# Trainium2, a two-block model on one core: in the seven-product projections the fifth product's low weight part made by VectorE, with other orders and the softmax scaling on ScalarE

## The chip, the cores and the metric

One core of one Trainium2 chip. The metric is the device time of one execution in microseconds (us); lower is better.

## The reference

Input x is 512 tokens by 2048 features. A first block (RWKV heads, pooled means, stick-breaking attention) and two further layers follow, then a last RMS norm. The change touches the last of these layers and the step behind it:

```
def odd_layer(x, norm_g, w_in, b_forget, w_out):
    hn = rmsnorm(x, norm_g)
    q, k, v, z, f_logit = split(hn @ w_in)
    log_f = log_sigmoid(f_logit + b_forget)
    o = forgetting_attention(q, k, v, log_f)     # 16 heads of 128
    o = o * silu(z)
    return x + o @ w_out
```

Per head, forgetting attention is softmax(q k^T / sqrt(128) + decay, causal) times v.

## The kernel before, in words

Everything is fp32. A product of a weight tile and the activations is made of three TensorE products: each operand is split into a high part (rounded to fp32r) and a low part (the rest), and high·high, low·high and high·low are added in PSUM. ScalarE makes a weight's high part (a copy, "cast" below), GpSimd or VectorE its low part (a subtraction of two tiles in SBUF, 128x1024; GpSimd does it as two instructions of 128x512).

In the odd layer, heads 1 to 15 get their four columns q, k, v, z by a block scheme with seven products instead of eight (`W7_`, lines 1930 to 2190). A **pair** is two of the four columns: the first pair (`pp` 0) is q and k, the second (`pp` 1) v and z. A pair has four weight blocks b11, b21, b12, b22 and seven products P0 to P6 (`w7_product`, matmuls at L2080, L2082 and L2083). Below, a name with a dash (P2') is of the second pair. The weights of the products are made in place, by these steps, each named in the code:

- `T1` to `T4` (L2147, L2151, L2153, L2157; VectorE): the sums of blocks that products 1, 2, 4 and 6 take.
- hi 0 to hi 6 (L2097, ScalarE): the casts. Cast 1 needs T1, cast 2 T2, cast 4 T3, cast 6 T4.
- low parts `l1`, `l2` on VectorE (L2163); lo 0, 3, 4, 5, 6 on GpSimd in that order (`w7_gpsimd`, L2174). T1 overwrites b11, so that it waits for lo 0.
- results: `x1`, `x5`, `x2`, `c21` (ScalarE, L2107, L2110, L2113, L2116) and `c12`, `c22`, `c11` (VectorE, L2129, L2132, L2135). P2 waits for x1, P3 for x5, P4 for x2, P5 for c12, P6 for c22: they leave the PSUM bank that the next product adds to.

A **unit** is one head's attention with the next head's two pairs woven in (`attention_tensor`, `attention_scalar`, `attention_vector`, lines 2193 to 2491); there are 15 units with products and a last one without. Every engine's order is written out by hand. TensorE's is: scores s (L2225), P0, transposes of v (`vt`, L2202), P1 to P4, the transposes of the softmax (`tp`, L2236), P5, P6, the output product (`pv`, L2244), P0' to P6'. VectorE's is: T2, the decay added to the scores and the mask (L2389, L2393), T3, l2, the row maxima (`largest`, L2399), T4, then `scaled`: v's low part `vl` (L2404), the reciprocal `rec` (L2406) and four multiplications of the exponentials by it (`sc0` to `sc3`, L2410); c12, c22, `pl` (L2414), T1', c11, l1', T2', T3', l2', `mix` (the head's gated output, L2422), T4', four steps that split q and k (`qh` to `kc`, L2381 and L2382), c12', c22', the next unit's T1, c11', l1. ScalarE's order is: cast 2, cast 3, x1, `vn` (L2268), x5, casts 4 and 5, four exponentials (L2274), x2, cast 6, cast 0', `pt` (L2279), cast 1', c21, casts 2' and 3', a wait for `mix` and the DMA that stores it (L2312), x1', cast 4', x5', cast 5', x2', cast 6', the next unit's cast 0, Silu (L2332), the next unit's cast 1, c21'.

The transposes `tp` wait for sc3. Weight blocks come by DMAs on SyncE's queue (`w7_sync`), each behind the step that frees its buffer.

Before unit 0, the activations of the products are summed (`fold_sums`) and split (`fold_round`, `fold_rest`, L1923); their low parts were made by VectorE for sums 1 and 3, by GpSimd for 2 and 4. Behind the last unit's products, two output tiles start early (`gemm_two`, L362 to L364, called by `early`): four weight parts cast by ScalarE (L2023), their low parts made by GpSimd (`out3_gpsimd`, L2031).

Of the kernel before, what the change touches and what calls it, by code (L numbers as in the profile page):

```python
# [181 lines left out]
def build_program(nc, stream, x, x_rows, params, consts, near_bias, lora, pool_w, s5_b, s5_c, out):  # L182
    with ExitStack() as ctx:
# [1673 lines left out]
        od_act = Steps(sem("od_act"), "vn e0 e1 e2 e3 pt gs")  # L1857
        od_dve = Steps(sem("od_dve"), "dc0 dc1 dc2 dc3 diag mx0 mx1 mx2 mx3 vl rec sc0 sc1 sc2 sc3 pl mix qh qc kh kc")
# [29 lines left out]
        for steps in (fold_sum, fold_act, fold_dve, fold_pool):  # L1888
            steps.start(0)
# [28 lines left out]
        def fold_rest(eng, steps, subtract, name, q):  # L1918

            fold_act.wait(eng, f"h{name}{q}", 0)  # L1920
            if name in "12":
                fold_sum.wait(eng, ("s2", "s4")[name == "2"] + str(q), 0)
            steps.mark(subtract(four(s_lo[name], q), four(s_raw[name], q), four(s_hi[name], q).bitcast(F32),  # L1923
                                ALU.subtract), f"l{name}{q}")

        def fold_gpsimd(pool, name, q):
            fold_rest(pool, fold_pool, nc.gpsimd.tensor_tensor, name, q)

        def fold_vector(dve, name, q):
            fold_rest(dve, fold_dve, nc.vector.tensor_tensor, name, q)  # L1930
# [6 lines left out]
        w7_prep = Steps(sem("w7_prep"), "T1 l1 T2 T3 l2 T4")  # L1937
# [29 lines left out]
        def w7_sync(sp):  # L1967
# [7 lines left out]
            def pair(u, pp):  # L1975
                p = at_pair(u, pp)
                if not first_pair(u, pp):
                    w7_prep.wait(sp, "T3", p - 1)
# [69 lines left out]
        def w7_product(pe, u, par, pp, i):  # L2048
# [4 lines left out]
            if i in (1, 2):  # L2053
                w7_prep.wait(pe, f"l{i}", p)
            else:
                pe.wait_ge(w7_lo, p * 5 + (W7_POOL.index(i) + 1))
# [11 lines left out]
            else:  # L2068
# [123 lines left out]
        def attention_tensor(pe):  # L2192
# [12 lines left out]
            def unit(u, par, more=True):  # L2205
# [167 lines left out]
        def attention_vector(dve):  # L2373
            A, V, S = od_act, od_dve, od_pe
            tt, ts = nc.vector.tensor_tensor, nc.vector.tensor_scalar
# [375 lines left out]
        def forget_vector(dve):  # L2751
# [630 lines left out]
        def _(pool):  # L3382
# [187 lines left out]
```

## Time and profile before

| what | value |
| --- | --- |
| median of 3 runs | 2985.13 us (2984.49 to 2986.8) |
| the profiled execution, its own time | 2987.02 us |
| its span in the trace | 2985.2 us |
| TensorE busy | 2895.5 us, 97% of the span |
| VectorE busy | 1637.2 us, 55% |
| ScalarE busy | 1302.0 us, 44% |
| GpSimd busy | 1436.1 us, 48% |

The timeline gives each instruction's start and duration from the span's start, and in brackets the idle time of its engine before it and what ended it. The attention with its seven-product pairs runs from 2055 to 2780 us of the span.

### The profile page before, as it was taken

The numbers are of one execution on the slowest core, as the hardware profiler recorded it, in microseconds if no ns is written. First come the engines' busy times: TensorE is split into PE (matmuls) and PEld (weight loads), VectorE is DVE, ScalarE is ACT, GpSimd is POOL, SyncE is SP. The second block draws the span as 40 slices with busy tenths as digits, with TensorE's granted clock in tenths as the row PEclk, the third lists the DMA queues.
The fourth block names the chain that finished last, engine by engine and source line by source line (L and its number), as shares of the span: only waits on it lengthen the run. The fifth ranks groups of instructions, "written<-read, shape, count | busy, mean of one in ns | idle before, by whom it ended". The sixth has DMA issues, their size and how long they took to land.

```text
span 2985.2 us, 52806 instructions
## 1 busy us (share of the span) xinstructions
PE 2895.5 (97%) x20478; PEld 2433.7 (82%) x20478; DVE 1637.2 (55%) x2091; ACT 1302.0 (44%) x1779; POOL 1436.1 (48%) x1037
## 2 busy tenths in 40 slices
PE   8999999999999999999999999998999999999998
PEld 6777777777777887777787777887999999999787
DVE  7555555334434128777823343139777777777412
ACT  5433444255655223333434563235555454545422
POOL 1222232433335446766643334447666666556643
PEclk9999999999999999999999999999999999999999
DMA  5111111222223433222242233432232322322433
GB/s 217 59 59 59 58 53 58 92 79 79 69 73 99 152 127 103 90 98 98 95 141 85 92 106 122 149 116 86 96 99 98 104 96 104 100 95 95 155 126 114
DMA packets 98561, 298.17 MB, mean 100 GB/s; under 512 B 10608, under 2 KB 16880, under 8 KB 97408
## 3 DMA queue, kind: packets, MB, share of 16 engines
q1 hardware_dynamic: 71440, 246.12, 24.3%
q10 hardware_dynamic: 26992, 50.22, 5.2%
q8 instruction: 95, 1.56, 0.2%
q14 instruction: 34, 0.28, 0.0%
HBM read 273.45 MB, written 22.84 MB: 99 GB/s over the span
## 4 chain that ended last, share of the span: by engine, by line
PE 75%; DVE 12%; issue 6%; ACT 3%; POOL 2%; DMA 0%; DVEq 0%; ACTq 0%; POOLq 0%; SPq 0%
PE ps L338 9%; PE ps L340 8%; PE ps L339 8%; PE ps L2080 5%; PE ps L2083 5%; PE ps L2082 5%; PE ps L1032 4%; PE ps L1033 4%; PE ps L1034 4%; PE ps L1352 3%; PE ps L1354 2%; PE ps L1353 2%; DVE arena L2410 2%; DVE arena L3206 1%; POOL w_lo L3392 1%
## 5 line engine op out<-in xcount | busy, mean ns | idle before, releaser
L3392 POOL TENSOR_TENSOR w_lo<-raw,w_hi 128x512 fp32r<-128x512 f32 x624 | 842.1, 1372 | 1221.9 <-ACT w_hi L765 1220.7
L338 PE MATMUL ps<-act_hi,w_hi 128*128 128x512 f32 x1232 | 485.9, 394 | 10.1 <-POOL w_lo L3392 4.1
L765 ACT ACTIVATE w_hi<-raw 128x1024 fp32r<-128x1024 f32 x316 | 333.2, 1055 | 356.1 <-PE ps L340 137.8
L340 PE MATMUL ps<-act_lo,w_hi 128*128 128x512 f32 x1232 | 480.9, 390 | 0.0
L339 PE MATMUL ps<-act_hi,w_lo 128*128 128x512 f32 x1232 | 480.7, 390 | 0.0
L2174 POOL TENSOR_TENSOR w_lo<-arena,w_hi 128x512 fp32r<-128x512 f32 x150 | 233.2, 1575 | 130.6 <-ACT w_hi L2097 130.6
L1032 PE MATMUL ps<-act_hi,w_hi 128*128 128x512 f32 x736 | 294.6, 400 | 0.0
L338 PEld LDWEIGHTS ps<-act_hi,w_hi 128*128 128x128 f32 x1232 | 231.8, 188 | 71.1 <-issue 15.1
L2174 POOL TENSOR_TENSOR w_lo<-raw,w_hi 128x512 fp32r<-128x512 f32 x150 | 222.2, 1506 | 135.7 <-ACT w_hi L2097 135.7
L1033 PE MATMUL ps<-act_hi,w_lo 128*128 128x512 f32 x736 | 287.2, 390 | 0.0
L1034 PE MATMUL ps<-act_lo,w_hi 128*128 128x512 f32 x736 | 287.0, 390 | 0.0
L2080 PE MATMUL ps<-act_hi,w_hi 128*128 128x256 f32 x960 | 273.7, 285 | 0.0
L2083 PE MATMUL ps<-mix_r,w_hi 128*128 128x256 f32 x960 | 273.0, 284 | 0.0
L2082 PE MATMUL ps<-act_hi,w_lo 128*128 128x256 f32 x960 | 271.7, 283 | 0.0
L340 PEld LDWEIGHTS ps<-act_lo,w_hi 128*128 128x128 f32 x1232 | 231.8, 188 | 48.9
L339 PEld LDWEIGHTS ps<-act_hi,w_lo 128*128 128x128 f32 x1232 | 231.8, 188 | 47.5 <-issue 0.7
L531 DVE TENSOR_TENSOR mix<-ps,arena 128x512 f32 (+1 forms) x46 | 31.7, 691 | 393.0 <-PE ps L340 369.0
L2083 PE MATMUL ps<-act_lo,w_hi 128*128 128x256 f32 x720 | 203.9, 283 | 0.0
L2083 PEld LDWEIGHTS ps<-mix_r,w_hi 128*128 128x128 f32 x960 | 185.6, 193 | 0.0
L2080 PEld LDWEIGHTS ps<-act_hi,w_hi 128*128 128x128 f32 x960 | 184.1, 192 | 0.7
L2082 PEld LDWEIGHTS ps<-act_hi,w_lo 128*128 128x128 f32 x960 | 184.1, 192 | 0.7
L1352 PE MATMUL ps<-act_hi,w_hi 128*128 128x512 f32 x384 | 168.9, 440 | 0.0
(498 smaller groups left out, 5982.7 us busy)
## 6 DMA issues: line engine op xcount, KB each, us to landing
raw<-stream SPq DMA_DIRECT2D x378, 512.0 KB, 3.3
arena<-stream SPq DMA_DIRECT2D x64, 512.0 KB, 3.9
residual<-mix ACTq DMA_DIRECT2D x32, 256.0 KB, 2.0
arena<-residual ACTq DMA_DIRECT2D x32, 256.0 KB, 2.7
arena<-x_rows SPq DMA_DIRECT2D x4, 1024.0 KB, 18.3
arena<-x ACTq DMA_DIRECT2D x16, 256.0 KB, 2.7
kept_qk<-mix ACTq DMA_DIRECT2D x16, 256.0 KB, 2.0
arena<-kept_qk ACTq DMA_DIRECT2D x16, 256.0 KB, 3.9
```

Of the source, the lines that this page charges most:

```text
L338: pe.matmul(dst, w_hi[:, slot, j, :], act_hi[:, a, :], start=first, stop=False)
L339: pe.matmul(dst, w_lo[:, slot, j, :], act_hi[:, a, :], start=False, stop=False)
L340: mm = pe.matmul(dst, w_hi[:, slot, j, :], act_lo[:, a, :], start=False, stop=last)
L765: nc.scalar.activation(w_hi[:, s, :, :], src[:, s % 2, :, :], ACT.Copy).then_inc(cast_done, 1)
L1032: self.pe.matmul(dst, w_hi[:, slot, j, :], act_hi[:, kt, :], start=kt == 0, stop=False)
L1033: self.pe.matmul(dst, w_lo[:, slot, j, :], act_hi[:, kt, :], start=False, stop=False)
L1034: mm = self.pe.matmul(dst, w_hi[:, slot, j, :], act_lo[:, kt, :], start=False, stop=kt == KT - 1)
L2080: pe.matmul(dst, w_hi[:, slot, j, :], hi[:, j, :], start=first and j == 0, stop=False, skip_group_check=True)
L2082: pe.matmul(dst, w_lo[:, slot, j, :], hi[:, j, :], start=False, stop=False, skip_group_check=True)
L2083: mm = pe.matmul(dst, w_hi[:, slot, j, :], lo[:, j, :], start=False, stop=j == HK - 1, skip_group_check=True)
L2174: last = nc.gpsimd.tensor_tensor(w_lo[:, slot, part, :], w7_buffer(pp, W7_SOURCE[i])[:, part, :], w_hi[:, slot, part, :].bitcast(F32), ALU ...
L3392: last = nc.gpsimd.tensor_tensor(w_lo[:, s, part, :], raw[:, s % 2, part, :], w_hi[:, s, part, :].bitcast(F32), ALU.subtract)
```

## The change

- In each pair, `l4` (the low part of product 4's weight) is made by VectorE between T3 and T4; GpSimd's list is 0, 3, 5, 6. The counts that SyncE, TensorE and VectorE wait for follow.
- On VectorE l2 now stands before T3, in both pairs. In the second pair the order is l2', T3', mix, l4', T4'.
- The four scalings sc0 to sc3 move to ScalarE, as copies with a scale from `at_st`, behind x2 and ahead of cast 6.
- ScalarE does an exponential of one column behind `vn`, so that the load of its function table stands there.
- All low parts of the sums before unit 0 are made by VectorE: 1 and 2 in `forget_vector`, 4 ahead of the first T1, 3 inside unit 0.
- For the early output tiles VectorE makes one of four low weight parts (`out3_vector`); GpSimd's order is 0, 3, 1; TensorE waits for two parts, not three, before it starts; SyncE's loads wait for the new counts.

```diff
@@ gemm_two
-                if j == 0:
+                if j == 0 and layer == 2:
+                    pe.wait_ge(split_done, n * 2 + (1, 4)[h])
+                    pe.wait_ge(at_first, 3)
+                elif j == 0:
                     pe.wait_ge(split_done, n * 2 + h + 3)
@@ fold_rest and its callers
-        fold_dve = Steps(sem("fold_dve"), "l10 l11 l30 l31")
-        fold_pool = Steps(sem("fold_pool"), "l20 l21 l40 l41")
+        fold_dve = Steps(sem("fold_dve"), "l10 l11 l20 l21 l40 l41 l30 l31")
@@ names of the pairs' steps
-        w7_prep = Steps(sem("w7_prep"), "T1 l1 T2 T3 l2 T4")
+        w7_prep = Steps(sem("w7_prep"), "T1 l1 T2 l2 T3 l4 T4")
-        W7_POOL = (0, 3, 4, 5, 6)
+        W7_POOL = (0, 3, 5, 6)
-        OUT3_ORDER = (0, 2, 3, 1)
+        OUT3_ORDER = (0, 3, 1)
@@ out3_vector
+            dve.wait_ge(out3_hi, 2)
+            nc.vector.tensor_tensor(w_lo[:, 2, :, :], OUT3_RAW[2], w_hi[:, 2, :, :].bitcast(F32),
+                                    ALU.subtract).then_inc(at_first, 1)
@@ attention_tensor, unit
-                V.wait(pe, "sc3", u)
+                A.wait(pe, "sc3", u)
@@ attention_scalar
+            def scaled(u):
+                V.wait(act, "rec", u)
+                for b in range(TB):
+                    o, w = AT_PLACE[b], (b + 1) * P
+                    A.mark(nc.scalar.activation(at_p[:, o:o + w], at_p[:, o:o + w], ACT.Copy,
+                                                scale=at_st[:, 2, b:b + 1]), f"sc{b}")
...
                 values(u)
+                nc.scalar.activation(norm_st[:, 0, 0:1], eps[:, 1:2], ACT.Exp)
                 out(0, "x5")
...
                 out(0, "x2")
+                scaled(u)
                 cast(0, 6)
@@ attention_vector, scaled
-                V.wait(dve, "rec", u)
-                for b in range(TB):
-                    o, w = AT_PLACE[b], (b + 1) * P
-                    V.mark(ts(at_p[:, o:o + w], at_p[:, o:o + w], at_st[:, 2, b:b + 1], None, ALU.mult), f"sc{b}")
@@ attention_vector, unit
+                prepare(u, par, 0, "l2")
                 prepare(u, par, 0, "T3")
-                prepare(u, par, 0, "l2")
+                largest(u)
                 if isinstance(u, int) and u == 0:
-                    fold_vector(dve, "3", 0)
-                    fold_vector(dve, "3", 1)
-                largest(u)
+                    fold_rest(dve, "3", 0)
+                    fold_rest(dve, "3", 1)
+                prepare(u, par, 0, "l4")
                 prepare(u, par, 0, "T4")
...
                 prepare(u, par, 1, "T2")
+                prepare(u, par, 1, "l2")
                 prepare(u, par, 1, "T3")
-                prepare(u, par, 1, "l2")
                 gated(u, at_gate)
+                prepare(u, par, 1, "l4")
                 prepare(u, par, 1, "T4")
@@ attention_vector, behind the last unit's products
-            out3_rest(dve, range(3))
+            out3_rest(dve, range(2))
+            out3_vector(dve)
+            out3_rest(dve, range(2, 4))
             decayed(u)
-            out3_rest(dve, range(3, 4))
             largest(u)
```

How the order moves. First VectorE, in a unit's second pair, from T1' on (L2147 before, L2151 now). Before:

```order
L2147 TENSOR_TENSOR arena<-arena 128x1024
L2134 REGISTER_ALU
L2135 SCALAR_TENSOR_TENSOR arena<-ps,w_x 128x256
L2162 ISA
L2163 TENSOR_TENSOR w_lo<-arena,w_hi 128x1024
L174 ISA
L2151 TENSOR_TENSOR arena<-raw,arena 128x1024
L2153 TENSOR_TENSOR arena<-raw,arena 128x1024
L2162 REGISTER_ALU
L2163 TENSOR_TENSOR w_lo<-arena,w_hi 128x1024
```

and now, from l1' to T4':

```order
L2167 TENSOR_TENSOR w_lo<-arena,w_hi 128x1024
L2155 TENSOR_TENSOR arena<-raw,arena 128x1024
L2166 REGISTER_ALU
L2167 TENSOR_TENSOR w_lo<-arena,w_hi 128x1024
L2157 TENSOR_TENSOR arena<-raw,arena 128x1024
L174 REGISTER_ALU
L174 ISA
L2428 TENSOR_TENSOR arena<-ps,arena 128x512
L2166 REGISTER_ALU
L2167 TENSOR_TENSOR w_lo<-arena,w_hi 128x1024
L174 REGISTER_ALU
L2161 TENSOR_TENSOR arena<-raw,arena 128x1024
```

T3' (L2153, now L2157) has gone behind l2' (L2163, now L2167), and between mix (L2428) and T4' (L2161) stands l4'.

Then ScalarE, in a unit's first pair, between the last exponential and cast 0' (L2101 is a cast, L2281 a scaling):

```order
L2274 ACTIVATE arena,at_st<-ps,at_st 128x512
L2264 ISA
L2264 DMA arena<-decays 128x512
L2117 ACTIVATE w_x<-ps 128x256
L174 REGISTER_ALU
L2281 ACTIVATE arena<-arena,at_st 128x128
L2281 ACTIVATE arena<-arena,at_st 128x256
L2281 ACTIVATE arena<-arena,at_st 128x384
L2281 ACTIVATE arena<-arena,at_st 128x512
L174 REGISTER_ALU
L2101 ACTIVATE w_hi<-raw 128x1024
```

Before, the cast stood directly behind x2 (L2113, now L2117).

## Rows read from the trace of the kernel before

**Rows 1.** The page: busy time of each engine (share of the span) and instructions
```profile
PE 2895.5 (97%) x20478; PEld 2433.7 (82%) x20478; DVE 1637.2 (55%) x2091; ACT 1302.0 (44%) x1779; POOL 1436.1 (48%) x1037
```

**Rows 2.** Waits of TensorE, 2055 to 2790: total us, times, longest us
```profile
PE ps L2080 <- DVE w_lo L2163: 18.5, 16, 6.9
PE ps L2236 <- DVE arena L2410: 11.4, 15, 1.2
```

**Rows 3.** Timeline, TensorE in unit 6: start us, us [idle before]
```profile
2356.77 0.28 PE L2082 MATMUL ps<-arena_r,w_lo 128*128 128x256 f32 x1
2356.89 0.28 PE L2083 MATMUL ps<-mix_r,w_hi 128*128 128x256 f32 x1
2357.99 0.38 PE L2080 MATMUL ps<-arena_r,w_hi 128*128 128x256 f32 x1 [0.82 <-DVE w_lo L2163]
...
2367.65 0.55 PE L2236 MATMUL ps<-ident,arena 128*128 128x128 f32 x3 [0.78 <-DVE arena L2410]
```

**Rows 4.** Timeline, VectorE in the same unit
```profile
2353.47 2.15 DVE L2153 TENSOR_TENSOR arena<-arena 128x1024 f32<-128x1024 f32 x1
2355.55 2.31 DVE L2163 TENSOR_TENSOR w_lo<-raw,w_hi 128x1024 fp32r<-128x1024 f32 x1
...
2363.18 4.41 DVE L2410 TENSOR_SCALAR arena<-arena,at_st 128x128 f32<-128x128 f32 x4
...
2371.68 1.22 DVE L2147 TENSOR_TENSOR arena<-arena 128x1024 f32<-128x1024 f32 x1
...
2376.50 1.22 DVE L2153 TENSOR_TENSOR arena<-raw,arena 128x1024 f32<-128x1024 f32 x1
2377.79 1.23 DVE L2163 TENSOR_TENSOR w_lo<-arena,w_hi 128x1024 fp32r<-128x1024 f32 x1
2378.93 0.68 DVE L2422 TENSOR_TENSOR arena<-ps,arena 128x512 f32<-128x512 f32 x1
2379.53 1.72 DVE L2157 TENSOR_TENSOR arena<-raw,arena 128x1024 f32<-128x1024 f32 x1
...
2385.87 1.67 DVE L2382 TENSOR_TENSOR arena_r<-arena,arena_r 128x512 fp32r<-128x512 f32 x1
...
2391.05 0.42 DVE L2132 TENSOR_TENSOR arena<-ps,w_x 128x256 f32<-128x256 f32 x1 [2.46 <-PE ps L2083]
```

**Rows 5.** Timeline, ScalarE in the same unit
```profile
2359.50 1.28 ACT L2274 ACT_TABLE_LOAD   x1
2360.79 0.37 ACT L2274 ACTIVATE arena<-ps,at_st 128x128 f32<-128x128 f32 x1
...
2362.16 0.69 ACT L2274 ACTIVATE arena<-ps,at_st 128x512 f32<-128x512 f32 x1
...
2380.24 0.38 ACT L2107 ACTIVATE w_x<-ps 128x256 f32<-128x256 f32 x1 [1.54 <-DVE arena L2422]
2380.52 1.05 ACT L2097 ACTIVATE w_hi<-arena 128x1024 fp32r<-128x1024 f32 x1
...
2382.41 0.39 ACT L2110 ACTIVATE w_x<-ps 128x256 f32<-128x256 f32 x1 [0.83 <-PE ps L2083]
```

**Rows 6.** Timeline, GpSimd in the same unit
```profile
2353.27 3.51 POOL L2174 TENSOR_TENSOR w_lo<-arena,w_hi 128x512 fp32r<-128x512 f32 x2 [7.24 <-ACT w_hi L2097]
...
2378.78 3.62 POOL L2174 TENSOR_TENSOR w_lo<-raw,w_hi 128x512 fp32r<-128x512 f32 x2 [8.81 <-ACT w_hi L2097]
...
2388.66 2.53 POOL L2174 TENSOR_TENSOR w_lo<-arena,w_hi 128x512 fp32r<-128x512 f32 x2
```

**Rows 7.** Timeline, TensorE in unit 0 and at the early output tiles
```profile
2069.52 0.58 PE L2080 MATMUL ps<-arena_r,w_hi 128*128 128x256 f32 x1 [6.86 <-DVE w_lo L2163]
...
2786.69 0.76 PE L362 MATMUL ps<-act_hi,w_hi 128*128 128x512 f32 x1 [6.03 <-issue]
```

**Rows 8.** Windows behind those waits: stretch, length, TensorE busy, granted clock, DMA share, GB/s
```profile
2786.60:2792.60 6.00, 5.91 (x14) 0.51 0.49 162
...
2069.40:2075.40 6.00, 5.88 (x27) 0.50 0.55 171
```

More of the change, by code:

```diff
@@ L1856, in build_program @@
         od_pe = Steps(sem("od_pe"), "s vt tp pv")
-        od_act = Steps(sem("od_act"), "vn e0 e1 e2 e3 pt gs")
-        od_dve = Steps(sem("od_dve"), "dc0 dc1 dc2 dc3 diag mx0 mx1 mx2 mx3 vl rec sc0 sc1 sc2 sc3 pl mix qh qc kh kc")
+        od_act = Steps(sem("od_act"), "vn e0 e1 e2 e3 sc0 sc1 sc2 sc3 pt gs")
+        od_dve = Steps(sem("od_dve"), "dc0 dc1 dc2 dc3 diag mx0 mx1 mx2 mx3 vl rec pl mix qh qc kh kc")
         def half_k(view, token_half):
@@ L1884, in build_program @@
         fold_act = Steps(sem("fold_act"), "h10 h20 h11 h21 h40 h41 h30 h31")
-        fold_dve = Steps(sem("fold_dve"), "l10 l11 l30 l31")
-        fold_pool = Steps(sem("fold_pool"), "l20 l21 l40 l41")
-        for steps in (fold_sum, fold_act, fold_dve, fold_pool):
+        fold_dve = Steps(sem("fold_dve"), "l10 l11 l20 l21 l40 l41 l30 l31")
+        for steps in (fold_sum, fold_act, fold_dve):
             steps.start(0)
@@ L1916, in fold_round, with fold_rest @@
             fold_act.mark(nc.scalar.activation(four(s_hi[name], q), four(s_raw[name], q), ACT.Copy), f"h{name}{q}")
-        def fold_rest(eng, steps, subtract, name, q):
-            fold_act.wait(eng, f"h{name}{q}", 0)
+        def fold_rest(dve, name, q):
+            fold_act.wait(dve, f"h{name}{q}", 0)
             if name in "12":
[L1922 to L1930, printed above, removed]
+                fold_sum.wait(dve, ("s2", "s4")[name == "2"] + str(q), 0)
+            fold_dve.mark(nc.vector.tensor_tensor(four(s_lo[name], q), four(s_raw[name], q),
+                                                  four(s_hi[name], q).bitcast(F32), ALU.subtract), f"l{name}{q}")
         w7_loaded = {b: sem("w7_loaded" + b) for b in ("11", "21", "12", "22")}
@@ L1978, in pair @@
                     w7_prep.wait(sp, "T3", p - 1)
-                    sp.wait_ge(w7_lo, p * 5 - 3)
+                    sp.wait_ge(w7_lo, p * 4 - 2)
                 fetch(p, "11", pp)
                 if not first_pair(u, pp):
-                    sp.wait_ge(w7_lo, p * 5 - 2)
+                    w7_prep.wait(sp, "l4", p - 1)
                 fetch(p, "12", pp)
                 if not first_pair(u, pp):
-                    sp.wait_ge(w7_lo, p * 5)
+                    sp.wait_ge(w7_lo, p * 4)
                 fetch(p, "21", pp)
@@ L2008, in out3_sync @@
                 if part == 1:
-                    sp.wait_ge(w7_lo, 5 * last + 3)
+                    w7_prep.wait(sp, "l4", last)
                     load_to(OUT3_RAW[1], N_OUT3, 1).then_inc(out3_loaded[1], 16)
-            sp.wait_ge(w7_lo, 5 * last + 5)
+            sp.wait_ge(w7_lo, 4 * last + 4)
             load_to(OUT3_RAW[2], N_OUT3 + 1, 0).then_inc(out3_loaded[2], 16)
@@ L2025, in out3_gpsimd @@
         def out3_gpsimd(pool):
-            for place, i in enumerate(OUT3_ORDER):
-                pool.wait_ge(out3_hi, place + 1)
+            for i in OUT3_ORDER:
+                pool.wait_ge(out3_hi, (1, 4, 2, 3)[i])
+                if i == OUT3_ORDER[-1]:
+                    pool.wait_ge(at_first, 3)
                 for k0 in (0, HK // 2):
@@ L2073, in w7_product @@
                 if first_pair(u, pp) and i < 4:
-                    fold_pool.wait(pe, ("l21", "l41")[i - 2], 0)
+                    fold_dve.wait(pe, ("l21", "l41")[i - 2], 0)
                 if first_pair(u, pp) and i == 4:
@@ L2464, in unit @@
                 V.finish()
+            fold_rest(dve, "4", 0)
+            fold_rest(dve, "4", 1)
             prepare(0, 0, 0, "T1")
@@ L2770, in forget_vector @@
                                          ALU.add).then_inc(fg.sem, 1)
-            fold_vector(dve, "1", 0)
-            fold_vector(dve, "1", 1)
+            for name in "12":
+                for q in range(2):
+                    fold_rest(dve, name, q)
         S5_TILES, S5_PAIRS, S5_J, S5_M = 8, 32, 4, P
@@ L3412, in _ @@
             rests(2 * (N_F + 2), 2 * N_OUT3)
-            fold_gpsimd(pool, "2", 0)
             w7_gpsimd(pool)
```

20 lines of the change are left out of this document (9 added, 11 removed).

## The prediction

> **What bounds the kernel now.** I read the page first: TensorE is busy for 97% of the span [rows 1], so that a step on another engine costs only where TensorE waits for it. Then the waits of TensorE over the attention: two kinds recur, about once in each of the 15 units: products (L2080) for a low part of VectorE (L2163), and the transposes tp (L2236) for a scaling (L2410) [rows 2]. The timeline of unit 6 shows both in place, 0.82 and 0.78 us [rows 3]. Matmuls start 0.12 us apart, so counted by starts the first wait costs 1.10 - 0.12 = 0.98 and, as its first matmul takes 0.38 for 0.28, 0.1 more; the second, counted in the same way (0.16 more than its idle time), 0.94. That is **2.0 us a unit**, all that a better order can win there. A third and a fourth place stand once each: 6.9 us in unit 0 and 6.0 us before the early output tiles [rows 7], each followed by a stretch at half clock [rows 8].
>
> The timelines of VectorE and GpSimd show the rule that decides this case. T3 takes 2.15 us and T3' 1.22 [rows 4]: T3 starts 0.2 us behind a GpSimd subtraction. Two such subtractions take 2.53 us alone and 3.51 beside T3 and l2 [rows 6]. So an instruction with two SBUF inputs on one engine waits until the other's has ended, and the one that asks first goes first. mix, which reads PSUM, takes 0.68 us and is not held although GpSimd has just started [rows 4, 6]. The Trainium skill says as much in "GPSIMD Engine Reference", Key points: GpSimd shares its SBUF interfaces with VectorE, with contention when a VectorE instruction has two SBUF inputs. It prices nothing, and speaks against work put on VectorE that has to be interleaved with GpSimd's.
>
> **The change, the first pair.** All times in this part are on unit 6's clock, with the unit begun at the same moment.
> - l2 before T3: l2 ends where T3 ended, 2355.6, or earlier. P2 wants it at 2357.0. The first wait goes.
> - GpSimd loses lo 4 and so starts lo 3 some 1.5 us earlier, ahead of l2 and T3; the two then take about 3.1 us for 4.4 [rows 4]. The maxima end near 2358.2.
> - The table load of 1.28 us leaves its place ahead of the exponentials and goes where ScalarE idles before x5. They start at 2359.5, where the load started, instead of 2360.8, and end at 2361.65 [rows 5].
> - l4 on VectorE, 1.23 us, from cast 4's end near 2358.6 (a cast is 1.05 us and cast 5 ends at 2359.5 [rows 5]) to 2359.8; one GpSimd half of lo 5 comes in between (1.15 us once it has its turn: lo 3' takes 3.62 less waits of 0.24 for l2' and 1.09 for T4', over two [rows 6]), T4 ends at 2362.05, vl and rec at 2362.8.
> - The four scalings leave VectorE, where they took 4.41 us with a GpSimd turn before each [rows 4]. On ScalarE the nearest rows are the four exponentials, 0.37 to 0.69 us, some 2.1 in all, less 0.3 of overlap [rows 5]: 1.83 us. They end at 2364.65, and TensorE wants tp at 2367.65 - 2.0 = 2365.65. The second wait goes, with 1.0 us to spare.
>
> So 2.0 us a unit are won by here.
>
> **The second pair.** The same edits push this part back. TensorE's own moments move 2.0 us forward; I count how late each step is against that.
> 1. The scalings stand ahead of cast 6 and cast 0'. Cast 6 ends at 2365.65, then lo 6 and lo 0' take 2 x 2.53 us [rows 6], so T1' starts at 2370.9. In step with TensorE it would be 2371.68 - 2.0 = 2369.7 [rows 4]. **1.2 us late.** (l4 is at no cost up to here: it is covered by the wait for cast 4 and the exponentials. The DMAs of the weight blocks land 4 us after lo 6 frees their buffer, before T2' needs them.)
> 2. l2' before T3'. Before, mix started 2378.93 - 2371.68 = 7.25 us after T1'; T3' ran from 2376.50 while cast 2' was made, and l2' at 2377.79 behind it [rows 4]. Now VectorE idles over cast 2' (1.2 us), does l2' in its old place, and T3' asks for SBUF 0.16 us after GpSimd has asked for lo 3' (2378.78, within l2' [rows 6]). So T3' waits a GpSimd half: l2' ends 7.34 us after T1', the half takes 1.16, T3' 1.09, mix starts at 9.5. **2.25 us later still**, 3.45 in all. ScalarE's x1' waits for mix and its DMA; it ended at 2380.63, and P1' at 2382.2 (x5' starts 0.2 behind it) [rows 5]: 1.5 us of cover with the semaphore's 0.1. P2', which waits for x1', starts 3.45 - 1.5 = **1.95 us late**.
> 3. l4' stands between mix and T4', and waits for cast 4', which ScalarE makes only behind x1'. Before, T4' started 0.6 us after mix did [rows 4]. Now: mix 0.68, to x1' 0.63, to cast 4' 0.28, cast 1.06, l4' 1.2: 3.85 us, **3.25 later**. From there to the end of kc (2387.54) it was 8.0 us with a GpSimd turn in front of each step; with lo 4' gone I count 7.5, since lo 5' and lo 6' still take four turns. c12' behind kc is 3.45 + 3.25 - 0.5 = 6.2 us late. It could have been done at 2388.0, and P4' ended at 2390.85 (c22' starts 0.2 behind it [rows 4]), so 2.75 us are covered: **P5' starts 3.45 us late**, the 1.95 of P2' included.
>
> A unit therefore gives 3.45 and gets 2.0: **+1.45 us**, and 14 units (1 to 14) **+20.3**.
>
> **The ends.** Unit 0: the wait of 6.86 us and the 2.7 behind it at half clock (27 matmuls in 5.9 us, 3.2 at 0.12) shrink, since GpSimd no longer makes sums' parts between T1 and T2 and l2 comes before T3, some 5 us earlier. Against that stand two sum parts and l4 ahead of T4 and tp, at 1.2 to 2.3 us each by the two durations of T3, then the second pair's 3.45. Between -5 and +5 I take **0**. The early tiles: TensorE waits for two parts, each on its own engine, and starts up to 6.0 us sooner; the 6 us at clock 0.51 [rows 8] would have been 3 at full. Of these 9.0 us some 3.3 go back, because VectorE's low activation parts and ScalarE's scalings then lead: **-5.7**, between -9 and -3. SyncE's order of loads stays and only gets new counts: nothing.
>
> **Sum.** 20.3 + 0 - 5.7 = +14.6 us. Against the profiled execution's own 2987.0 that is 3001.6; that execution lies 1.9 us above the median of 2985.1, so the median goes to **2999.7**. A measurement of this kernel can tell about 0.2%, 6 us, from no change.
>
> **Rivals.**
> - T3' gets its turn before lo 3' (the requests are 0.16 us apart, and no row shows so close a race; far apart, the first goes first). Step 2 is 1.16 us shorter, a unit costs +0.3: 4 - 5.7 = -2, 2983. Chance 0.17.
> - Faster: the cover in the second pair is larger than I read it, because x1' no longer meets its DMA or the splits of q and k run without GpSimd's turns. The turns in front of the four splits are worth 4 x 1.16 = 4.6 us, more than the 3.45; it decides when cast 6' comes so late that GpSimd stands idle there. For it: GpSimd loses 2.5 us a pair. Against it: cast 5' and cast 6' do not wait for l4'. All waits gone gives 14 x -2.0 - 5.7 and some 4 in unit 0: -38, 2947. Chance 0.15; partly so, 2955 to 2979, 0.11.
> - GpSimd's lo 5' gets ahead of T4', 0.12 us apart: +1.1 a unit, 3015. Chance 0.10.
> - The clock: after 6.9 us of waiting the clock is 0.50, after 0.8 us it stays [rows 3, 8]. If the new waits of 2.0 and 1.5 us were enough, each of the units would pay 2.7 us as unit 0 did: +38, 3038. Chance 0.03. In the Trainium skill, "TensorE: Matmul & The Clock Gate", Part 1, the clock follows how busy TensorE has been of late; by that alone neither outcome is excluded, and the rows decide for no fall.
> - The change not doing what it says: the order printed shows each step moved, so I leave no chance there.
>
> **How the numbers follow.** The forecast, slower by two new waits, has 0.44. Slower by over 0.2%: 0.44 + 0.10 + 0.03 = 0.57. Within 0.2%: the first rival, 0.17. Faster: 0.26. The range leaves out the full gain and the clock: 2955 to 3015. The forecast's own range is 2990 to 3012.
>
> **What would show it.** Of the profile after: no wait of a product for L2167 in the first pair and none of L2236; instead, in each unit, P2' waiting some 2.0 us for ScalarE's x1' (L2111), and P5' some 1.5 us for VectorE's c12' (L2133); T3' at 2.3 us; scalings of 0.37 to 0.69 us each; a period between units 1.4 us longer; T1' 1.2 us later behind tp (5.2 us after it for 4.0). The early tiles starting right behind the transposes of v at full clock. I am wrong if P2' and P5' start without idle time: then the cover was larger, and the 2.0 us a unit stay won.

## The result and the profile after

| what | before | after |
| --- | --- | --- |
| median of 5 runs each, side by side | 2985.13 us (2983.83 to 2986.8) | 2999.86 us (2998.36 to 3000.11) |
| ratio, 95% interval | | 1.0051 (1.0039 to 1.0062) |
| span of the profiled execution | 2985.2 us | 2997.6 us |

The change makes the kernel 0.5% slower. The forecast was 2999.7 us. Line numbers have moved: L2080 is now L2084 (the products), L2163 is L2167 (low parts on VectorE), L2147, L2151, L2153 and L2157 (T1 to T4) are L2151, L2155, L2157 and L2161, L2174 (GpSimd) is L2178, L2107 and L2129 (x1, c12) are L2111 and L2133, L2422 (mix) is L2428. The scalings are L2281, on ScalarE.

The page of the changed kernel, busy times (answers to [rows 1]):

```profile
PE 2902.0 (97%) x20478; PEld 2440.1 (81%) x20478; DVE 1612.3 (54%) x2062; ACT 1330.7 (44%) x1858; POOL 1346.0 (45%) x971
```

GpSimd has lost 90 us of work, VectorE 25, ScalarE has got 29; TensorE's share stays at 97%. What has changed stands in its waits from 2055 to 2790 us (answers to [rows 2]):

```profile
PE ps L2084 <- ACT w_x L2111: 26.7, 15, 1.9
PE ps L2084 <- DVE arena L2133: 11.4, 9, 1.3
PE ps L2084 <- DVE w_lo L2167: 3.9, 2, 2.0
```

The last row is unit 0 alone: P2 waits 1.98 us for l2, and P4 1.88 us for l4. In the units behind it the wait for l2 is gone, and so is that of tp for a scaling. P2' waits for x1' and P5' for c12' instead. The timeline of TensorE in the unit that answers to the one of [rows 3]:

```profile
2388.70 0.36 PE L2084 MATMUL ps<-arena_r,w_hi 128*128 128x256 f32 x1 [1.84 <-ACT w_x L2111]
...
2398.85 0.38 PE L2084 MATMUL ps<-act_hi,w_hi 128*128 128x256 f32 x1 [1.29 <-DVE arena L2133]
```

VectorE in the same unit (answers to [rows 4]), from T1 of the first pair to T1 of the next unit:

```profile
2351.49 1.23 DVE L2151 TENSOR_TENSOR raw<-arena,raw 128x1024 f32<-128x1024 f32 x1 [1.17 <-POOL w_lo L2178]
...
2357.69 1.69 DVE L2399 TENSOR_TENSOR ps<-ps,arena 128x128 f32<-128x128 f32 x4 [1.29 <-PE ps L2225]
...
2360.03 2.19 DVE L2167 TENSOR_TENSOR w_lo<-raw,w_hi 128x1024 fp32r<-128x1024 f32 x1
2362.14 1.21 DVE L2157 TENSOR_TENSOR arena<-arena 128x1024 f32<-128x1024 f32 x1
...
2365.13 1.23 DVE L2167 TENSOR_TENSOR w_lo<-arena,w_hi 128x1024 fp32r<-128x1024 f32 x1 [0.18 <-ACT w_hi L2101]
2366.27 2.32 DVE L2161 TENSOR_TENSOR raw<-raw 128x1024 f32<-128x1024 f32 x1
...
2377.42 1.23 DVE L2151 TENSOR_TENSOR arena<-arena 128x1024 f32<-128x1024 f32 x1 [1.16 <-POOL w_lo L2178]
...
2383.54 1.23 DVE L2167 TENSOR_TENSOR w_lo<-arena,w_hi 128x1024 fp32r<-128x1024 f32 x1 [1.20 <-ACT w_hi L2101]
2384.68 2.32 DVE L2157 TENSOR_TENSOR arena<-raw,arena 128x1024 f32<-128x1024 f32 x1
2386.92 0.68 DVE L2428 TENSOR_TENSOR arena<-ps,arena 128x512 f32<-128x512 f32 x1
2389.53 1.23 DVE L2167 TENSOR_TENSOR w_lo<-arena,w_hi 128x1024 fp32r<-128x1024 f32 x1 [1.93 <-ACT w_hi L2101]
2390.68 1.22 DVE L2161 TENSOR_TENSOR arena<-raw,arena 128x1024 f32<-128x1024 f32 x1
...
2398.37 0.42 DVE L2133 TENSOR_TENSOR arena<-ps,w_x 128x256 f32<-128x256 f32 x1 [0.19 <-DVE arena_r L2392]
...
2400.69 1.23 DVE L2151 TENSOR_TENSOR raw<-arena,raw 128x1024 f32<-128x1024 f32 x1 [1.57 <-POOL w_lo L2178]
```

L2399 is the decay: VectorE waits 1.29 us for the scores (L2225) before it. T3' (at 2384.68) takes 2.32 us: GpSimd asked 0.14 us sooner, as its row shows (answers to [rows 6]):

```profile
2384.54 3.59 POOL L2178 TENSOR_TENSOR w_lo<-raw,w_hi 128x512 fp32r<-128x512 f32 x2 [7.25 <-ACT w_hi L2101]
```

And ScalarE (answers to [rows 5]): the table load ahead of x5, the four scalings, and x1' behind mix:

```profile
2361.52 1.28 ACT L2305 ACT_TABLE_LOAD   x1
...
2369.31 1.92 ACT L2281 ACTIVATE arena<-arena,at_st 128x128 f32<-128x128 f32 x4 [0.95 <-DVE at_st L2416]
...
2388.17 0.38 ACT L2111 ACTIVATE w_x<-ps 128x256 f32<-128x256 f32 x1 [3.71 <-DVE arena L2428]
```

**Where the time came from.** The first transpose tp of units 0, 1, 14 and 15 (the last has no products of its own), before and then after:

```profile
2081.53 1.31 PE L2236 MATMUL ps<-ident,arena 128*128 128x128 f32 x10 [0.42 <-DVE arena L2410]
...
2129.22 1.31 PE L2236 MATMUL ps<-ident,arena 128*128 128x128 f32 x10 [0.98 <-DVE arena L2410]
...
2749.19 1.31 PE L2236 MATMUL ps<-ident,arena 128*128 128x128 f32 x10 [1.19 <-DVE arena L2410]
...
2800.41 1.25 PE L2236 MATMUL ps<-ident,arena 128*128 128x128 f32 x10
```

```profile
2077.02 1.34 PE L2236 MATMUL ps<-ident,arena 128*128 128x128 f32 x10
...
2126.09 1.26 PE L2236 MATMUL ps<-ident,arena 128*128 128x128 f32 x10
...
2765.43 1.25 PE L2236 MATMUL ps<-ident,arena 128*128 128x128 f32 x10
...
2812.28 1.31 PE L2236 MATMUL ps<-ident,arena 128*128 128x128 f32 x10 [0.23 <-ACT arena L2281]
```

| stretch of the span | forecast, us | measured, us |
| --- | --- | --- |
| to tp of unit 1 (unit 0, the first pair of 1) | 0 - 2.0 | 2126.09 - 2129.22 = -3.1 |
| 13 units, tp of 1 to tp of 14 | 13 x 1.45 = +18.9 | 639.34 - 619.97 = +19.4 |
| tp of 14 to tp of 15 (second pair of 14, early tiles) | 3.45 - 5.7 = -2.3 | 46.85 - 51.22 = -4.4 |
| from there to the end | 0 | 185.3 - 184.8 = +0.5 |
| sum | +14.6 | +12.4 (medians: +14.7) |

The 6.03 us wait at the early tiles is gone; waits of 0.23 and 0.66 us stand in its place.

### The profile page after: what moved, and what is told of

It reads as the page before. It is cut to its first block, busy times and chain, and to the rows that moved or that the text cites. A ratio compares the mean times of both kernels' runs of the same rounds, so it can differ in the third digit from the quotient of the medians.

```text
span 2997.6 us, 52652 instructions
## 1 busy us (share of the span) xinstructions
PE 2902.0 (97%) x20478; PEld 2440.1 (81%) x20478; DVE 1612.3 (54%) x2062; ACT 1330.7 (44%) x1858; POOL 1346.0 (45%) x971
## 4 chain that ended last, share of the span: by engine, by line
PE 57%; issue 17%; POOL 13%; DVE 10%; ACT 2%; DMA 1%; DVEq 0%; POOLq 0%; ACTq 0%; SPq 0%
POOL w_lo L2178 11%; PE ps L338 8%; PE ps L340 8%; PE ps L339 8%; PE ps L1035 4%; PE ps L1037 4%; PE ps L1036 4%; PE ps L1355 3%; PE ps L1357 3%; PE ps L1356 3%; POOL w_lo L3404 1%; DVE arena L3218 1%; PE ps L1420 1%; PE ps L1087 1%; DVE arena L3248 1%
## 5 line engine op out<-in xcount | busy, mean ns | idle before, releaser
L3404 POOL TENSOR_TENSOR w_lo<-raw,w_hi 128x512 fp32r<-128x512 f32 x624 | 845.0, 1377 | 1217.3 <-ACT w_hi L768 1215.7
L338 PE MATMUL ps<-act_hi,w_hi 128*128 128x512 f32 x1232 | 486.4, 395 | 10.3 <-POOL w_lo L3404 4.4
L2178 POOL TENSOR_TENSOR w_lo<-raw,w_hi 128x512 fp32r<-128x512 f32 x150 | 251.3, 1696 | 265.9 <-ACT w_hi L2101 265.9
L1035 PE MATMUL ps<-act_hi,w_hi 128*128 128x512 f32 x736 | 294.2, 400 | 0.0
L2084 PE MATMUL ps<-act_hi,w_hi 128*128 128x256 f32 x960 | 275.3, 287 | 14.4 <-DVE arena L2133 12.5
L339 PEld LDWEIGHTS ps<-act_hi,w_lo 128*128 128x128 f32 x1232 | 232.1, 188 | 47.7 <-issue 0.7
L2084 PEld LDWEIGHTS ps<-act_hi,w_hi 128*128 128x128 f32 x960 | 184.2, 192 | 17.3 <-DVE arena L2133 13.1
L2178 POOL TENSOR_TENSOR w_lo<-arena,w_hi 128x512 fp32r<-128x512 f32 x90 | 123.8, 1397 | 109.6 <-ACT w_hi L2101 109.6
L2084 PE MATMUL ps<-arena_r,w_hi 128*128 128x256 f32 x480 | 142.1, 296 | 28.9 <-ACT w_x L2111 26.7
```

The lines of the kernel that those rows point to most:

```text
L338: pe.matmul(dst, w_hi[:, slot, j, :], act_hi[:, a, :], start=first, stop=False)
L339: pe.matmul(dst, w_lo[:, slot, j, :], act_hi[:, a, :], start=False, stop=False)
L1035: self.pe.matmul(dst, w_hi[:, slot, j, :], act_hi[:, kt, :], start=kt == 0, stop=False)
L2084: pe.matmul(dst, w_hi[:, slot, j, :], hi[:, j, :], start=first and j == 0, stop=False, skip_group_check=True)
L2178: last = nc.gpsimd.tensor_tensor(w_lo[:, slot, part, :], w7_buffer(pp, W7_SOURCE[i])[:, part, :], w_hi[:, slot, part, :].bitcast(F32), ALU ...
L3404: last = nc.gpsimd.tensor_tensor(w_lo[:, s, part, :], raw[:, s % 2, part, :], w_hi[:, s, part, :].bitcast(F32), ALU.subtract)
```

## The experiments

The diffs leave out lines that only rename or recount steps. The experiments came in three groups: the first four test terms of the prediction, the next four what those left, the last three a second theory. The kernel before, run beside each group, took 2984.27, 2984.13 and 2984.42 us.

**e1_t3_first: T3' ahead of l2' again, in the second pair alone** (edit to the changed kernel; that pair's list of step names, not shown, follows it)

```diff
+                prepare(u, par, 1, "T3")
                 prepare(u, par, 1, "l2")
-                prepare(u, par, 1, "T3")
```

> The changed kernel with T3' ahead of l2' again, in the second pair alone. Theory (the order and a GpSimd turn make mix 2.25 us later, and with it x1'): P2' no longer waits, since mix is then 1.2 us late behind a cover of 1.5; P5' waits about 1.2 us (1.2 + 3.25 - 0.5 - 2.75), for 3.5 in all in the changed kernel. A unit loses 2.25 us, 14 units 31: 2968 us. Rival (the late T1', scalings ahead of the casts on ScalarE, is what costs): the order is worth at most the 0.16 us race, under 0.5 us a unit: 2993 us or more, and P2' goes on waiting some 1.5 us.

2966.93 us, ratio 0.9941 (0.9926 to 0.9956). As expected: the wait of P2' is gone, that of P5' is left. This single swap is the difference between slower and faster.

```profile
PE ps L2085 <- DVE arena L2134: 16.0, 15, 1.2
```

**e2_x1_first: in the changed kernel, x1' and cast 4' ahead of ScalarE's wait for mix and its DMA**

```diff
+                out(1, "x1")
+                cast(1, 4)
                 V.wait(act, "mix", u)
                 act.dma_start(mixed[...], at_gate)
-                out(1, "x1")
-                cast(1, 4)
```

> The changed kernel with x1' and cast 4' on ScalarE ahead of the wait for mix and its DMA; VectorE's order as changed. Theory: P2' no longer waits (x1' only needs P0'), l4' can start some 0.4 us behind mix instead of 1.9, so c12' is 4.75 us late behind a cover of 2.75: P5' waits 2.0 us, the unit is 1.45 us shorter than in the changed kernel: 14 units 20, 2979 us. Rival (a longer mix path is harmless, VectorE is simply too full in the second pair): P5' takes over the whole 3.4 us and the time stays at 2997 to 3000.

2980.47 us, ratio 0.9988 (0.9979 to 0.9997), as expected. P2' waits no longer, P5' waits 1.9 us a unit.

**e3_both: the two edits above together**

> Both edits: T3' ahead of l2', and x1' and cast 4' ahead of the wait for mix. Theory: mix 1.2 us late, T4' 1.8 us later behind it, 0.5 less of GpSimd: c12' 2.5 us late behind a cover of 2.75, so neither P2' nor P5' waits and the 3.4 us a unit are gone: 14 units 47.6, 2952 us, faster than the kernel before by 1.1%. Rival (VectorE too full): at least 1 us a unit stays at P5', 2966 us or more.

2961.04 us, ratio 0.9921 (0.9906 to 0.9936): between the two. A wait of P5' that should have gone is left, 0.7 us in each of 15 units:

```profile
PE ps L2085 <- DVE arena L2134: 10.6, 15, 1.3
```

**b1_tiles: the early output tiles' part alone, in the kernel before** (`gemm_two`, `out3_vector` and its callers, as in the change's diff)

```diff
-        OUT3_ORDER = (0, 2, 3, 1)
+        OUT3_ORDER = (0, 3, 1)
...
-            out3_rest(dve, range(3))
+            out3_rest(dve, range(2))
+            out3_vector(dve)
+            out3_rest(dve, range(2, 4))
```

> The kernel before with the early output tiles' part of the change alone (VectorE makes one of the four low parts, TensorE waits for two). Theory: the wait of 6.0 us goes and with it the half clock behind it, some 3 us come back as waits of the transposes and of act_lo: -5.7 us, 2979.4. Rival (the tiles only start sooner and then wait for the last unit's softmax, whose chain is unchanged): 0 to -2 us, 2983 to 2985.

2980.37 us, ratio 0.9987 (0.9978 to 0.9996): 3.9 us won for the 5.7 forecast. With the scalings still on VectorE the transposes tp get a wait there:

```profile
2793.56 1.31 PE L2247 MATMUL ps<-ident,arena 128*128 128x128 f32 x10 [1.60 <-DVE arena L2421]
```

**e4_c12: c12' ahead of the split of k, in the changed kernel**

```diff
                 split(at_q_in, at_q, at_q_lo, done(("qh", "qc")))
+                w7_sum_out(dve, u, 1, "c12")
                 split(at_k_in, at_k, at_k_lo, done(("kh", "kc")))
-                w7_sum_out(dve, u, 1, "c12")
```

> The changed kernel with one step moved: in the second pair VectorE makes c12' ahead of the split of k, not behind it. My theory: P5' waits 1.5 us a unit only because c12' stands behind four splits on VectorE (qh, qc, kh, kc); with two of them behind it, it is ready some 3 us sooner, before P5' wants it, and the scores of the next unit, which want k, come only behind P5' and P6'. The wait of P5' goes, that of P2' for x1' (2.0 us) stays: 14 x 1.5 = 21 us less, 2979 us (ratio to the kernel before 0.998). Rival: what holds P5' is the end of x2', c22' or the low parts lo 5' and lo 6' of GpSimd, hidden behind c12' now; then the wait only changes its name and the time stays within 5 us of 3000.

2997.30 us, ratio 1.0045 (1.003 to 1.006). A miss of 18 us, and the most telling run. The wait of P5' did go, but that of P2' grew, from 26.7 to 35.2 us:

```profile
PE ps L2084 <- ACT w_x L2111: 35.2, 15, 3.1
```

Against the changed kernel 2.6 us are won by the medians and 1.8 by the two ratios, whose intervals overlap: it can't be told from nothing. So P5''s 1.5 us a unit could not be had by moving c12' alone: TensorE only came sooner to the next wait.

**e5_all: the three edits of e1_t3_first, e2_x1_first and e4_c12 together**

> The changed kernel with T3' ahead of l2', x1' and cast 4' ahead of ScalarE's wait for mix, and c12' ahead of the split of k, all in the second pair. Beside it the first two alone gave 2961.0 us, with a wait of P5' for c12' of about 0.7 to 0.9 us a unit left. My theory: this last wait goes too, 14 x 0.9 = 12 us less: 2949 us (ratio 0.988), and the products of the units 1 to 14 wait for nothing above 0.3 us. Rival: the wait moves on to P6' for c22', since c22' stands behind the split of k now (two splits, about 3 us, later behind c12'), and half of it or more stays: 2955 us or above.

2956.96 us, ratio 0.991 (0.9894 to 0.9925). Neither theory: no wait above 0.3 us is left in units 1 to 14, nor has P6' one, yet a unit takes 46.28 us, 0.66 more than TensorE needs (below). 4 us were won, not 12.

**b3_scale: the scalings and the one-column exponential alone, in the kernel before**

```diff
-                V.wait(pe, "sc3", u)
+                A.wait(pe, "sc3", u)
...
+                nc.scalar.activation(norm_st[:, 0, 0:1], eps[:, 1:2], ACT.Exp)
                 out(0, "x5")
...
                 out(0, "x2")
+                scaled(u)
                 cast(0, 6)
```

> The kernel before with one part of the change: the four scalings and the one-column exponential on ScalarE; orders of low parts and l4 on GpSimd as before. My theory: the transposes tp no longer wait (0.94 us a unit), T1' comes some 1.2 us later behind the scalings, which the 1.5 us of cover in the second pair still hold, and P2 still waits 1.0 for l2: 14 x 0.94 = 13 us less, 2971 us (ratio 0.9956). Rival: the cover of x1' and of c12' is smaller than the 1.5 and 2.75 us that I read (another run showed the latter 0.9 too large), so that the 1.2 us show as a new wait of P2' or P5' of 0.5 us or more: 2978 us or above.

2972.80 us, ratio 0.9962 (0.9949 to 0.9975), as expected: of the change's parts this one is worth 11 us.

**b2_fold: the sums' low parts alone, in the kernel before**

```diff
-        fold_dve = Steps(sem("fold_dve"), "l10 l11 l30 l31")
-        fold_pool = Steps(sem("fold_pool"), "l20 l21 l40 l41")
+        fold_dve = Steps(sem("fold_dve"), "l10 l11 l20 l21 l40 l41 l30 l31")
...
+            fold_vector(dve, "4", 0)
+            fold_vector(dve, "4", 1)
             prepare(0, 0, 0, "T1")
```

> The kernel before with one part of the change: all low parts of the sums before unit 0 made by VectorE, none by GpSimd. My theory: it acts on unit 0 alone. GpSimd's lo parts in unit 0 start sooner, the wait of 6.9 us for l2 shrinks by 2 to 5 us, and some of it comes back where VectorE's l1, T1 and T2 stand behind the added parts: between -4 and +1 us, middle -1.5, 2982.8 us. Rival: the parts of sum 4 ahead of the first T1 stand on the path into the attention (P0 and P1 of unit 0 start 2 to 4 us later): +2 to +5 us, 2987 or above. Units 1 to 14 as before under both.

2981.78 us, ratio 0.9993 (0.9984 to 1.0002): within the first theory's range, but not told from nothing. The longest wait for l2 fell from 6.9 to 4.2 us, and tp of unit 0 came 0.9 us sooner.

**A second theory: the ring.** e4_c12 shows what was wrong with counting wait by wait. Each helper engine waits for another: the scalings for T4 ahead of them on VectorE (in the kernel before for the exponentials), T1' for GpSimd's lo 0', x1' for mix behind T3', the next T1 for lo 0 behind lo 5' and lo 6'. That is a closed ring of VectorE, ScalarE and GpSimd. It touches TensorE at two places: the decay waits for the scores, and pl, behind which T1' stands, waits for tp by way of ScalarE's `pt`. If the ring turns more slowly than TensorE works, it sets the period, and TensorE's waits are only what is left of it, wherever the order puts them.

Which of two links comes last differs from kernel to kernel. In the kernel before, the decay starts when T2 ends, with no wait for the scores, T1' starts when pl ends, with no wait for lo 0', and GpSimd works from lo 3' (2378.78) to the end of lo 0 (2393.69) without a gap, so that x1' is not in the ring; T1 waits for lo 0:

```profile
2351.13 1.69 DVE L2389 TENSOR_TENSOR ps<-ps,arena 128x128 f32<-128x128 f32 x4
...
2370.27 1.49 DVE L2414 TENSOR_TENSOR arena_r<-ps,arena_r 128x1280 fp32r<-128x1280 f32 x1 [2.01 <-ACT arena_r L2279]
...
2393.83 1.23 DVE L2147 TENSOR_TENSOR raw<-arena,raw 128x1024 f32<-128x1024 f32 x1 [2.36 <-POOL w_lo L2174]
...
2391.15 2.54 POOL L2174 TENSOR_TENSOR w_lo<-raw,w_hi 128x512 fp32r<-128x512 f32 x2
```

In the changed kernel T1' does wait for lo 0' (1.16 us), and the decay waits 1.2 to 1.3 us for the scores in every unit from the third on. The scores come behind x1', cast 4', l4', T4', the four splits, c12', P5' and P6'; T1 is earlier than it need be by that wait. Here, then, TensorE works within the ring, at P5', P6' and the scores; P2' and tp are no part of it.

The four stretches of the ring are read off the starts of T1, the first scaling, T1', x1' and the next T1, which stand in the rows above for the changed kernel: 17.82, 8.11, 10.75 and 12.52 us, in all 49.20. The same for all kernels (median over the units from the third on):

| kernel | T1 to scalings | to T1' | to x1' | to next T1 | period, mean |
| --- | --- | --- | --- | --- | --- |
| before | 17.04 | 8.50 | 8.57 | 13.59 | 47.69 |
| changed | 17.84 | 8.12 | 10.75 | 12.52 | 49.23 |
| e1_t3_first | 17.87 | 8.11 | 8.51 | 12.52 | 47.01 |
| e2_x1_first | 17.84 | 8.11 | 6.94 | 14.89 | 47.79 |
| e3_both | 17.87 | 8.11 | 6.94 | 13.69 | 46.60 |
| e4_c12 | 17.50 | 8.18 | 10.75 | 12.54 | 49.05 |
| e5_all | 17.40 | 8.14 | 6.94 | 13.70 | 46.27 |
| b3_scale | 15.60 | 8.99 | 8.57 | 13.59 | 46.75 |
| e6_cast6 | 18.12 | 6.59 | 10.74 | 12.52 | 47.98 |
| b4_l2 | 17.51 | 8.45 | 8.56 | 13.60 | 48.13 |
| e7_all | 18.08 | 6.59 | 7.84 | 13.11 | 45.62 |

Beside an edit within it, a stretch keeps its length to 0.1 us from kernel to kernel, whatever the waits of TensorE are; only the first is some 0.4 us shorter in e5_all, and in e4_c12 in the units whose scores come sooner (17.4 to 17.5; 17.8 in the others). There the decay starts 4.9 us after T1, not 6.2, without a wait, but then T3 has to wait for GpSimd's lo 3 and takes 2.31 us, not 1.21, so that 0.9 of the 1.3 us are lost again. From e4_c12, in such a unit:

```profile
2307.93 1.69 DVE L2399 TENSOR_TENSOR ps<-ps,arena 128x128 f32<-128x128 f32 x4
...
2312.51 2.31 DVE L2157 TENSOR_TENSOR arena<-arena 128x1024 f32<-128x1024 f32 x1
```

In e7_all x1' waits for TensorE, so that its last stretches are not the ring's own any more. The last three rows were run to test the theory.

**e6_cast6: cast 6 ahead of the scalings, in the changed kernel**

```diff
+                cast(0, 6)
                 scaled(u)
-                cast(0, 6)
```

> The changed kernel with cast 6 ahead of the four scalings on ScalarE, not behind them. My theory (step 1 of the prediction: the scalings ahead of cast 6 make T1' late): cast 6 runs when T4 is done, 2.4 us sooner, lo 6 and lo 0' end and T1' starts 2.0 us sooner; P2' no longer waits for x1' (2.0 us a unit), P5' still waits 1.3 to 1.5 for c12', the scalings end 0.4 us later, within the 0.8 us that the transposes tp leave: 14 x 2.0 = 28 us less, 2972 us (ratio to the kernel before 0.996). Rival: lo 0' is what T1' waits for and it starts only behind cast 0', so that T1' gains 1 us or less: 2985 us or above. Second rival: tp waits for the scalings now, by 0.5 us or more a unit: 2979 or above.

2981.03 us, ratio 0.9989 (0.998 to 0.9999): between theory and rivals. The stretch from the scalings to T1' shrank by 1.5 us, not 2.0: T1' stands right behind pl, which waits for tp by way of ScalarE, and starts when pl ends, as in the kernel before:

```profile
2367.09 1.49 DVE L2420 TENSOR_TENSOR arena_r<-ps,arena_r 128x1280 fp32r<-128x1280 f32 x1 [1.94 <-ACT arena_r L2286]
2368.50 1.22 DVE L2151 TENSOR_TENSOR arena<-arena 128x1024 f32<-128x1024 f32 x1
```

The period fell by 1.25 us, as the ring's two stretches say (-1.53 + 0.28). P2' still waits 0.6 us, P5' 1.3.

**e7_all: the four edits of e1_t3_first, e2_x1_first, e4_c12 and e6_cast6 together**

> The changed kernel with T3' ahead of l2', x1' and cast 4' ahead of the wait for mix, c12' ahead of the split of k, and cast 6 ahead of the scalings. Without the last it took 2957.0 us, 46.28 us a unit, with waits of 0.2 to 0.3 us each at tp, P5' and P2 left; TensorE by itself needs some 45.75 (47.69 of the kernel before less its 2.0 of waits). Theory (the other three engines form a ring, each step waiting for another of them, x1' to T1 to the scalings to T1' and back to x1', which turns in 46.3 us): cast 6 ahead of the scalings makes the ring 2 us shorter, and TensorE is the bound: 14 x 0.5 = 7 us less, 2950 us (ratio 0.9885). Rival (each wait is fixed by its own neighbours): T1' is not waited for any longer, so its coming sooner buys nothing, and the scalings, 0.4 us later, make tp wait 0.4 more: 2960 to 2963 us.

2947.12 us, ratio 0.9876 (0.9859 to 0.9892), 1.2% faster than the kernel before and, by the two ratios, 1.7% faster than the changed one. The view of TensorE's waits is empty from 2080 to 2700 us, and the period is 45.62 us in each: TensorE's own. The ring, which had turned in 46.28, was the bound in e5_all, though there P2' and T1' were not late for anybody. Moving cast 6 could win only if it was.

**b4_l2: l2 ahead of T3 in the first pair alone, in the kernel before**

```diff
+                prepare(u, par, 0, "l2")
                 prepare(u, par, 0, "T3")
-                prepare(u, par, 0, "l2")
```

> The kernel before with one edit: in the first pair l2 stands ahead of T3 on VectorE. It tests whether the 2.0 us of waits a unit are two waits that can be won one by one. Theory of the prediction: P2's wait for l2 (1.08 us) goes, the wait of tp for the scalings stays 0.94: 14 x 1.08 = 15 us less, and some 2 us in unit 0: 2968 us (ratio 0.9945). Rival (the ring: the scalings come when the other engines have turned, whatever TensorE does, since each wait ahead is cover for the next): the wait of tp grows by most of what P2's loses, up to 2.0 us, and the time is 2979 us or above (ratio 0.998 or above).

2990.02 us, ratio 1.0017 (1.0007 to 1.0027): slower, where the prediction's way of counting says 15 us faster. The wait of P2 for l2 is gone in units 1 to 14, and two others have taken its place (waits of TensorE, 2055 to 2790 us):

```profile
PE ps L2237 <- DVE arena L2411: 19.0, 15, 2.1
PE ps L2081 <- ACT w_x L2114: 10.6, 14, 0.9
PE ps L2081 <- DVE w_lo L2164: 5.0, 2, 4.7
```

tp waits 19.0 us for 11.4, P4 waits for x2, 10.6 us, which stands behind the exponentials on ScalarE. T3 ends later, and so do cast 4, the exponentials and the scalings: the ring has become 0.4 us longer, and with it each unit.

**The clock bears the ring out.** In the changed kernel TensorE's clock fell behind the wait of P2' in 5 of the units 1 to 14, and not in the others. Two units, 5 us each from P2' on (length, TensorE busy, PEld, VectorE, ScalarE, GpSimd, granted clock, DMA share, GB/s):

```profile
2191.80:2196.80 5.00, 4.99 (x29) 5.00 (x30) 4.12 (x4) 2.67 (x5) 2.89 (x2) 0.66 0.72 259
2241.00:2246.00 5.00, 4.97 (x41) 5.00 (x42) 4.10 (x4) 3.39 (x5) 2.86 (x2) 1.00 0.72 259
```

In the first TensorE does 12 matmuls fewer: at 0.12 us each 1.4 us are lost. In these five units P5' does not wait for c12' (it waits 1.1 to 1.3 us of idle time in all nine others), and tp follows tp by 49.2 us there as elsewhere. TensorE can lose 1.4 us in such a unit at no cost, because P5' would have had to wait for c12' as long.

## Why the prediction was right, and where it was not

The time (2999.7 against 2999.86 us) and the two new waits with their places and sizes came as forecast. The mechanism held too; what did not hold is a way of counting that the prediction uses, and that its own sum does not need.

- **The first pair.** Both waits went. Scalings 1.92 us (forecast 1.83), 1.0 us before tp starts (1.0). l2 and T3 took 3.3 us (3.1), T4 met lo 5 and took 2.32.
- **Step 1**: T1' starts 5.2 us behind tp, as forecast. e6_cast6 showed the cause: with cast 6 first it comes 1.5 us sooner.
- **Step 2**: mix starts 2386.92 - 2377.42 = 9.50 us after T1'; forecast 9.5. The rival in which T3' wins its turn did not occur. e1_t3_first took the swap back and won 33 us.
- **Step 3**: mix to T4' 3.76 us (3.85), T4' to the end of kc 7.5 (7.5).
- **The waits**, counted as [rows 3] were: P2' 2.0 us (1.95), P5' 1.45 (1.5). A unit became 1.49 us longer over 13 units (1.45).
- **Step by step on the path.** Where the decay waits for the scores, T1 is early, so the fair mark for a unit's start is the decay. Medians over the units, kernel before and changed: decay to the scalings 12.05 and 11.62 us, scalings to T1' 8.50 and 8.12, T1' to x1' 8.57 and 10.75, x1' to the next decay 18.57 and 18.74. T1' thus comes 0.81 us sooner (forecast 0.8: 1.2 late against 2.0), x1' another 2.18 later (2.25), and from x1' on 0.17 are added (0: 3.25 - 0.5 - 2.75). The sum, +1.54, against +1.45: no large errors that cancel.
- **What did not hold: waits as separate prices.** "A unit therefore gives 3.45 and gets 2.0" is true as a balance: these waits came and those went. But 2.0 stands in both numbers (the 3.45 is counted against moments moved forward by 2.0), and neither can be had wait by wait. e4_c12 took away the 1.5 of P5' and won 2.6 us in all where the same counting said 21; b4_l2 took away the 1.08 of P2 and lost 5.6 where it said 15 to be won. They missed by 18 and 22 us. In the kernel before, P2 and tp both wait on the way from the scores to the last scaling, so that the wait taken from the one is added to the other; the change won there because it made that stretch itself shorter.
- **e3_both and e5_all** missed for the same reason: with T3' and x1' put right, the ring (46.60, then 46.28 us) stayed above TensorE's 45.62. But "all that a better order can win there", 2.0 us a unit, was right: 47.69 - 45.62 = 2.07, and e7_all won it.
- **Unit 0** gave -3.1 with the first pair of unit 1, for -2.0; its own tp came 4.5 us sooner. **Early tiles**: 3.9 us alone for 5.7; in the changed kernel the stretch gave 4.4 where 2.3 was forecast with a full second pair's delay in it. How much of that delay shows there was not measured apart. That the medians agree to 0.2 us is luck: the stretches of the table are off by -1.1, +0.5, -2.1 and +0.5 us, and the spans of the two profiled executions differ by 2.3 us less than the medians.
- **The clock**: the rival priced a fall at 2.7 us a unit in each. It fell in 5 units of 14, for 1.4 us each, and was hidden by the wait of P5'.

## What to carry to other kernels

Before you price the waits of the busiest engine one by one, see whether the other engines form a ring that closes from one iteration to the next, with the busiest engine in it at a place or two at most. The sign of it: steps of the helper engines keep their distances from kernel to kernel, and a wait taken from the busiest engine turns up at another place. If the ring's length is the period, the waits are what is left over, and only an edit that shortens the ring counts: add up what it does to each stretch between steps that wait for another helper engine, and compare the sum with the busiest engine's own time per iteration. Check at each step which of its inputs comes last: an edit can move that to another input, and then only part of it is won. Here TensorE's 97% hid a ring of 47.7 us against its own 45.6.

## What the runs showed of the hardware beyond that

- In these rows the turns on SBUF between VectorE and GpSimd went to whoever asked first, even 0.14 us apart: T3', asked for at 2384.68, was held while GpSimd's half begun at 2384.54 ran, and took 2.32 us. Where VectorE came 0.12 us sooner (T4' at 2390.68, lo 5' at 2390.80) it ran in 1.22 us. The Trainium skill ("GPSIMD Engine Reference", Key points) names the contention for an instruction of VectorE with two SBUF inputs, and the runs agree.
- Behind a wait of TensorE of 1.84 us the granted clock fell for some 3.3 us in 5 of 14 units of the same program (matmuls 0.21 us apart, not 0.12), with nothing in the rows to tell those units from the rest; in unit 0, behind waits of 1.98 and 1.88 us, the granted clock was 0.56 and 0.70 over 3 us. Behind the two waits of 0.8 us a unit in the kernel before it stayed at 1.00 in all units from 1 to 14.
- In e4_c12 it fell in 6 of the units 1 to 14. Since the ring and not TensorE set the period, the next unit's wait for x1' was shorter behind each of them, 1.4 to 1.9 us, as in the first of these rows, behind the fall in the unit begun before it; behind a unit at full clock it was 2.3 to 3.1 us, as in the second.

```profile
2290.99 0.36 PE L2084 MATMUL ps<-arena_r,w_hi 128*128 128x256 f32 x1 [1.83 <-ACT w_x L2111]
...
2340.01 0.35 PE L2084 MATMUL ps<-arena_r,w_hi 128*128 128x256 f32 x1 [2.81 <-ACT w_x L2111]
```
